# The mixture-of-experts layer of a two-block network on one core: four blocks of program joined into one, and the first weights loaded earlier

## The reference, cut to what matters

```python
h = h + expert_choice_ffn(rms_norm(h, norm2_w), w_router, w_gate, w_up, w_down)
h = rms_norm(h, final_norm_w)

def expert_choice_ffn(n, w_router, w_gate, w_up, w_down):
    cap = 2 * L // N_EXPERTS                                  # 64
    aff = softmax(einsum('bld,de->ble', n, w_router))         # over 16 experts
    vals, idx = lax.top_k(swapaxes(aff, 1, 2), cap)           # 64 tokens for each expert
    xs = n[idx]                                               # [16, 64, 1024]
    y = einsum(silu(einsum(xs, w_gate)) * einsum(xs, w_up), w_down) * vals[..., None]
    return zeros((L, D)).at[idx].add(y)
```

## Time and profile before

| what | value |
|---|---|
| median of 3 runs | 3746.36 us (3746.19 to 3746.59) |
| span of the profiled execution | 3742.8 us, of which 3.6 us less than the median of the runs |
| PE busy | 3347.0 us (89% of the span) |
| DVE, ACT, POOL busy | 1713.9, 1074.5, 305.7 us |
| read from HBM | 320.17 MB, 86 GB/s over the span |
| w_experts slabs | 96, of 1024 KB each |

### The profile page before, as it was taken

One profiled execution on the slowest core, in us unless ns is written; L12 is line 12 of the kernel. 1 busy time (PEld: TensorE's weight loads), 2 busy tenths in 40 slices (PEclk: granted clock), 3 DMA queues, 4 the chain that ended last, 5 costly groups with the idle time before them and its releaser, 6 DMA issues. The chain is left out here.

```text
span 3742.8 us, 39198 instructions
## 1 busy us (share of the span) xinstructions
PE 3347.0 (89%) x15374; PEld 2407.1 (64%) x15374; DVE 1713.9 (46%) x2459; ACT 1074.5 (29%) x1530; POOL 305.7 (8%) x260
## 2 busy tenths in 40 slices
PE   6999999879958776999998899998999998889997
PEld 3476574635744234888774468887888784568886
DVE  3758657556340014442436744423442326744433
ACT  3322231123220014222222632223222213642222
POOL 3212210012010001000002000000000002000001
PEclk8999999989969997999999999999999998999998
DMA  2101000000227972222310022222222311022221
GB/s 87 46 24 46 23 24 34 35 23 1 90 81 294 420 296 69 101 92 99 110 71 6 1 102 100 99 92 81 101 94 97 111 43 44 1 90 101 91 100 56
DMA packets 50838, 325.16 MB, mean 87 GB/s; under 512 B 7056, under 2 KB 7568, under 8 KB 13328
## 3 DMA queue, kind: packets, MB, share of 16 engines
q1 hardware_dynamic: 50704, 323.34, 23.0%
HBM read 320.17 MB, written 2.10 MB: 86 GB/s over the span
## 5 line engine op out<-in xcount | busy, mean ns | idle before, releaser
L364 PE MATMUL psum<-ffn_x_hi,ffn_w_hi 128*128 128x512 f32 x1408 | 548.2, 389 | 1.4 <-DVE ffn_x_lo L320 1.3
L364 PE MATMUL psum<-ffn_x_hi,ffn_w_lo 128*128 128x512 f32 x1408 | 547.7, 389 | 0.0
L364 PE MATMUL psum<-ffn_x_lo,ffn_w_hi 128*128 128x512 f32 x1408 | 547.7, 389 | 0.0
L309 DVE TENSOR_TENSOR ffn_w_lo<-ffn_raw,ffn_w_hi 128x2048 fp32r<-128x2048 f32 x128 | 293.4, 2292 | 420.3 <-ACT ffn_w_hi L280 420.3
L280 ACT ACTIVATE ffn_w_hi<-ffn_raw 128x2048 fp32r<-128x2048 f32 x128 | 245.2, 1916 | 564.3 <-PE psum L364 564.3
L104 PE MATMUL psum<-mix_normed,mix_ring 128*128 128x512 f32 x832 | 366.7, 601 | 13.0 <-DVE recurrences_work L1226 8.3
L364 PEld LDWEIGHTS psum<-ffn_x_hi,ffn_w_hi 128*128 128x128 f32 x1408 | 264.4, 188 | 61.8 <-DVE ffn_w_lo L316 6.8
L364 PEld LDWEIGHTS psum<-ffn_x_lo,ffn_w_hi 128*128 128x128 f32 x1408 | 264.4, 188 | 54.7
L364 PEld LDWEIGHTS psum<-ffn_x_hi,ffn_w_lo 128*128 128x128 f32 x1408 | 264.3, 188 | 54.6
L104 PEld LDWEIGHTS psum<-mix_normed,mix_ring 128*128 128x128 f32 x832 | 159.5, 193 | 214.3 <-issue 213.6
L364 PE MATMUL psum<-ffn_hid_hi,ffn_w_hi 128*128 (+1 forms) x704 | 273.9, 389 | 0.0
(11 more groups left out here) (477 smaller groups left out, 5407.9 us busy)
## 6 DMA issues: line engine op xcount, KB each, us to landing
ffn_raw<-w_ffn SPq DMA_DIRECT2D x128, 1024.0 KB, 4.8
mix_ring<-w_experts SPq DMA_DIRECT2D x48, 1024.0 KB, 13.6
mix_ring<-w_mix SPq DMA_DIRECT2D x32, 1024.0 KB, 7.5
mix_normed<-w_experts SPq DMA_DIRECT2D x24, 1024.0 KB, 13.6
experts_slabs<-w_experts SPq DMA_DIRECT2D x24, 1024.0 KB, 13.6
mix_ring<-w_gdn SPq DMA_DIRECT2D x16, 1024.0 KB, 4.9
mix_ring<-w_ssd SPq DMA_DIRECT2D x10, 1024.0 KB, 4.8
mix_ring<-w_out SPq DMA_DIRECT2D x7, 1024.0 KB, 7.4
```

The lines of the kernel that those rows point to most:

```text
L309: dve.tensor_tensor(w_lo[:, q, :], raw[:, q, :], w_hi[:, q, :].bitcast(F32), ALU.subtract)\
L364: ins = pe.matmul(out, wp[:, q, w], xp, start=start and a == 0, stop=stop and a == 2)
```

## The change

The stages `norm2`, `route`, `pick` and `experts` become one block, `experts`.

- **Norm.** The factor 1/rms is a number for each token. Where tokens lie on the partitions it is one column, `rstd` of 128x4. PE makes its sums by four products of one column (L1754); it is multiplied in where the turned tiles leave PSUM (L1836 on ACT, L1881 on DVE) and on the logits (L1885). ACT and DVE only multiply the residual's tiles by the gain, four each (L1828, L1869). The turning of the tiles (L1763) now comes ahead of the logits.
- **Picking in four groups.** `pick` is built and used for four experts (256 columns) at a time: DVE by 4 instructions of 128x256 a group (L1907), PE by 64 products of 256 columns (L1680). Group 0 comes ahead of the first pair. Groups 1 to 3 are cut in four parts of 16 products each, and `aside` puts two parts into each of the pairs 0 to 5. The turns for `put` go into the pairs 6 and 7 in the same way. The weighing stands between the gate and the up products of pair 0.
- **Eleven early slabs.** SP issues nine slabs at the start of the block: six into the ring and its extra slots, three into the memory of `y`, whose later rows aren't written until these are read. Two more follow into the memory of `m.xT` when the logits are done. The 85 others wait for `used` as before, on a ring of 8 slots.
- The buffers that only the mixer uses are given free ahead of the layer (`head_memory`), which makes the room. The scatter is the same.

The core of the diff:

```diff
-    with stage(nc, m, "route") as (block, sem):
...
-            for n in range(SLOTS):
-                fetch(sp, n)
...
-    with stage(nc, m, "pick") as (block, sem):
...
-                    for part in (x_hi, x_lo):
-                        ins = pe.matmul(m.ps[:, 4 + n % 4, :], part[:, t, tok(k)], pick[:, t, half * T:(half + 1) * T],
...
-        @block.sync
-        def _(sp):
-            for n in range(n_early, 12 * pairs):
-                if n >= slots:
-                    sp.wait_ge(used, (n - slots) // 2 + 1)
-                sp.dma_start(ring[n % slots], io["w_experts"][n]).then_inc(landed[n % slots], 16)
...
+    @block.sync
+    def _(sp):
+        sp.dma_start(router, io["w_router"]).then_inc(loaded, 16)
+        for n in range(n_first):
+            sp.dma_start(slots[n], io["w_experts"][n]).then_inc(landed[n], 16)
+        for n in range(n_over):
+            sp.dma_start(over[n], io["w_experts"][n_first + n]).then_inc(over_landed[n], 16)
+        sp.dma_start(m.rope_tables, io["const_f"][:, m.rope_at:m.rope_at + m.rope_width]).then_inc(tables, 16)
+        sp.wait_ge(logits, 1)
+        for n in range(n_first + n_over, n_early):
+            sp.dma_start(slots[slot(n)], io["w_experts"][n]).then_inc(landed[slot(n)], 16)
+        for n in range(n_early, 12 * pairs):
+            before = n - n_slots if n >= n_early + n_slots else \
+                slot(n) if slot(n) < n_first else slot(n) + n_over
+            sp.wait_ge(used, before // 2 + 1)
+            sp.dma_start(slots[slot(n)], io["w_experts"][n]).then_inc(landed[slot(n)], 16)
+        sp.wait_ge(tables, 16)
...
+        def gather(g, j, bank):
+            for k in (2 * j, 2 * j + 1):
+                for t in range(NT):
+                    for part in (x_hi, x_lo):
+                        ins = pe.matmul(m.ps[:, bank, k % 2 * wide:(k % 2 + 1) * wide], part[:, t, tok(k)],
+                                        pick[:, t, g * wide:(g + 1) * wide],
+                                        start=(t == 0 and part is x_hi), stop=(t == NT - 1 and part is x_lo))
+            ins.then_inc(gathered, 1)
+
+        def turn_picks(pair):
+            for t in range(NT):
+                ins = pe.transpose(m.ps[:, 7, tok(t)], pick[:, t, tok(pair)].bitcast(F32), m.ident)
+            ins.then_inc(put_done, 1)
+
+        def aside(i, spot):
+
+            if i < 2 * (groups - 1):
+                g, j = i // 2 + 1, 2 * (i % 2) + spot // 2
+                if spot == 0:
+                    pe.wait_ge(read_a, 2 + i)
+                    pe.wait_ge(picked, NT * (g + 1))
+                    gather(g, j, 7)
+                elif spot == 2:
+                    pe.wait_ge(read_v, 3 + i)
+                    gather(g, j, 7)
+                return
+            done = 2 * (i - 2 * (groups - 1))
+            if spot == 0:
+                pe.wait_ge(*((put_a, done) if done else (read_a, 2 * groups)))
+            elif spot < 3:
+                pe.wait_ge(put_v, done + spot)
+            else:
+                pe.wait_ge(put_a, done + 1)
+            turn_picks(2 * done + spot)
...
+        for t in range(NT):
+            ins = pe.matmul(m.ps[:, 7, t:t + 1], m.squares[:, tok(t)], m.ones[:, 0:1], start=True, stop=True)
+        ins.then_inc(summed, 1)
+        for n in range(2 * NT):
+            half, t = divmod(n, NT)
+            pe.wait_ge(x_by_act, 2 * half + 2)
+            pe.wait_ge(x_by_dve, 2 * half + 2)
+            if n >= 6:
+                pe.wait_ge(split, n - 5)
+            for k in range(4):
+                ins = pe.transpose(m.ps[:, turn_bank(n), tok(k)], m.xT[:, 4 * half + k, tok(t)], m.ident)
+            ins.then_inc(tok_turned, 1)
+        pe.wait_ge(loaded, 16)
+        for t in range(NT):
+            ins = product(pe, m.ps[:, 6, t * NE:(t + 1) * NE], lambda k: m.xT[:, k, tok(t)],
+                          lambda k: router[:, k, :])
+        ins.then_inc(logits, 1)
+        pe.wait_ge(normed, 1)
+        pe.wait_ge(split, 2 * NT)
+        for t in range(NT):
+            ins = pe.transpose(m.ps[0:NE, 0, tok(t)], affinity[:, t, :], m.ident)
+        ins.then_inc(aff_turned, 1)
+        pe.wait_ge(placed, 1)
+        for t in range(NT):
+            ins = pe.transpose(m.ps[:, 1, t * NE:(t + 1) * NE], chosen[:, tok(t)], m.ident[0:NE, 0:NE])
+        ins.then_inc(back, 1)
+        pe.wait_ge(picked, NT)
+        for j in range(4):
+            gather(0, j, 4 + j)
+        for i in range(pairs + 1):
+            if i < pairs:
+                if i >= 2:
+                    pe.wait_ge(hidden, i - 1)
+                for s in range(2):
+                    if i == 0:
+                        pe.wait_ge(read_v, s + 1)
+                        pe.wait_ge(read_a, s + 1)
+                    elif i % 2 == 0:
+                        pe.wait_ge(read_v, i + 2)
+                        pe.wait_ge(read_a, i + 2)
+                    gate_or_up(i, 0, s)
+                    aside(i, s)
+            if i == 0:
+                weigh()
+            else:
+                turn(i - 1)
+            if i < pairs:
+                for s in range(2):
+                    gate_or_up(i, 1, s)
+                    aside(i, 2 + s)
+            if i:
+                pe.wait_ge(turned_read, i)
+                if i >= 2:
+                    pe.wait_ge(y_read, i - 1)
+                for s in range(2):
+                    down(i - 1, s)
...
+            act.activation(x_hi[:, t, half * T:(half + 1) * T], m.ps[:, turn_bank(n), :], ACT.Copy,
+                           scale=rstd[:, t:t + 1]).then_inc(hi_done, 1)
...
+        def picks(g):
+            e = NE // groups
+            for t in range(NT):
+                dve.tensor_tensor(pick[:, t, g * wide:(g + 1) * wide].rearrange("p (e s) -> p e s", e=e),
+                                  m.slot.unsqueeze(1).to_broadcast([P, e, CAP]),
+                                  slot_of[:, t, g * e:(g + 1) * e].unsqueeze(2).to_broadcast([P, e, CAP]),
+                                  ALU.is_equal).then_inc(picked, 1)
+
+        picks(0)
+        for j in (0, 2):
+            take(0, j, 4 + j)
+        for g in range(1, groups):
+            picks(g)
+        for i in range(pairs):
+            if i < 2 * (groups - 1):
+                take(i // 2 + 1, 2 * (i % 2), 7)
...
-            resid_norm_stage(nc, m, "norm2", m.gains["norm2"], m.xT)
-            with expert_memory(nc, m):
-                experts(nc, m, io)
+            experts(nc, m, io)
```

More of the change, by code:

```diff
@@ L1775, in experts @@
-    picking.close()
-    y = slabs.enter_context(nc.sbuf_tensor("experts_y", [P, NE // 2, D], F32))
-    extra = parts.enter_context(nc.sbuf_tensor("experts_slabs", [P, 2, SLAB], F32))
-    ring += [extra[:, s, :] for s in range(2)]
-    hid, silu, hid_t = (cut(small, 2 * T * n, 2, T) for n in range(3))
-    slots = len(ring)
-    pairs = NE // 2
-    with stage(nc, m, "experts") as (block, sem):
-        landed = sem(slots)
-        used, silued, hidden, turned, turned_read, y_read = sem(6)
+    pairs, groups = NE // 2, NE // 4
@@ new lines, in experts, with sb, slot @@
+    wide = 2 * P
+    with ExitStack() as ctx:
+        def sb(what, *shape, dt=F32):
+            return ctx.enter_context(nc.sbuf_tensor(f"experts_{what}", [P, *shape], dt))
+        pick, tok_hi, tok_lo = (sb(what, 4096, dt=F32R) for what in ("pick", "tok_hi", "tok_lo"))
+        pick = cut(pick, 0, NT, NE * CAP)
+        x_hi, x_lo = (cut(buf, 0, NT, D) for buf in (tok_hi, tok_lo))
+        put = cut(tok_hi, 0, pairs, T)
+        y_hi, y_lo = (cut(tok_lo, 2048 * n, 2, pairs, P) for n in range(2))
+        gathered_x = sb("xs", 2 * KD * wide)
+        xs = [cut(gathered_x, g * KD * wide, KD, wide) for g in range(2)]
+        y = sb("y", pairs, D)
+        extra = sb("slabs", 2, SLAB)
+        small = sb("small", 4 * T + 320)
+        hid, hid_t = (cut(small, 2 * T * n, 2, T) for n in range(2))
+        silu = cut(m.norm_tmp, 0, 2, T)
+        rest, chosen, ones_row, count = (cut(small, T * n, T)[0:NE] for n in (2, 3, 0, 1))
+        at = 4 * T
+        affinity, slot_of, router = cut(small, at, NT, NE), cut(small, at + 64, NT, NE), cut(small, at + 128, KD, NE)
+        peak, total, rstd = (cut(small, at + 256 + 4 * n, NT) for n in range(3))
+        top, weight = cut(small, at + 272, 8)[0:NE], cut(small, at + 280, pairs)
+        spare = m.xT[:, :, :].rearrange("p k t -> p (k t)")
+        lent = y[:, :, :].rearrange("p i d -> p (i d)")
+        slots = [m.ring[:, s, :] for s in range(SLOTS)] + [extra[:, s, :] for s in range(2)] + \
+                [spare[:, s * SLAB:(s + 1) * SLAB] for s in range(2)]
+        over = [lent[:, (s + 1) * SLAB:(s + 2) * SLAB] for s in range(3)]
+        n_slots, n_over, n_first = len(slots), len(over), 6
+        n_early = n_slots + n_over
+        by_expert = lambda a: a.unsqueeze(2).to_broadcast([P, NT, NE])
+        def slot(n):
+            return n if n < n_first else n - n_over if n < n_early else (n - n_early) % n_slots
@@ L1788, in experts @@
```

(20 more changed lines are left out.)

448 lines of the change are left out of this document (181 added, 267 removed).

## The result

The changed kernel takes **3694.43 us** (median of 4 runs, 3688.53 to 3699.28), the kernel before in the same comparison 3746.28 us (3741.26 to 3746.59). The ratio is 0.9867 with the interval [0.9852, 0.9881], a gain of 51.9 us against the 51.1 that were forecast. The profiled execution took 3690.96 us, with a span of 3689.2. Run and span are thus 1.8 us apart, as in every other execution that has both; the 3.6 us given for the kernel before compare its span with the median of other executions.

A forecast was written before the change was run, and what follows sets the result against it. The layer was taken as a chain of small steps, then a stream bound by transfers. Used 6 at 1130.3 + 2.3 + 78 x 2.492 = 1327.0 instead of 1378.1, 51.1 us less: 3746.4 - 51.1 = 3695.3 us, range 3686 to 3709.

The forecast's parts named there:

- U6: End of the expert step on PE that raises `used` to 6, releasing slabs 18 and 19; forecast at 1130.3.
- softmax, picking, numbers: Between logits and picking matrix: 19.0 us before, plus one instruction of 0.23 us and two handovers, 19.3 us.
- picking matrix of group 0: DVE ahead of the gathering: 4 instructions of 256 columns at 0.4 us each, without a barrier, done at 1080.7.
- gathering of group 0: PE ahead of the first expert step: 64 products at 0.127 us plus 2.6 us for the clock, 10.7 us.
- weighing, and the step behind it: PE in pair 0, ahead of used 3: weighing 9.6 us, then a step of 3.55 us plus 1.8 for the clock.
- Turns: The 32 turns at the block's start, from 1043.5: their old 6.63 us, ending at 1050.1.
- Cold logits: Rival: the clock doesn't rise behind the turns, logits take 13.84 us instead of 9.6, 4.2 us more; chance 0.2.
- Serial loads: Rival: weight loads don't overlap in the gathering, 0.22 us a product, 11.8 us more, 3707.1 us; chance 0.12.
- The lower bound of 6.1 us: Least time for the logits' 32 products, all at clock 1.00, from 21 records in 2 us, two a product.
- the rival of the warm start: Logits and weighing both at 1.00 throughout, 3.5 us less each: 8.8 us less in all, 3686.5 us; chance 0.08.
- The idle queue: Between 1095.0 and 1130.3 the transfer queue moves only 7 slabs (17 us) and idles for some 16 us.
- 2.3 + 78 x 2.492 behind used 6: Stream's end: 2.3 us extra landing time, then 78 slabs left at 2.492 us each; last slab at 1327.0.

The follow-up runs named there:

- weigh one pair: Changed kernel with 28 of the weighing's 32 products left out, for timing only: 3684.71 us, layer 276.97 us.
- weigh spread: Changed kernel with the weighing cut into four runs of 8 products, one behind each gate and up step of pair 0: 3689.39 us, layer 281.71 us.
- narrow weighing: Changed kernel with the weighing in four runs and in reduced precision, affinities split into rounded part and rest: 3686.12 us, layer 278.77 us.
- the repeat: The changed kernel, unchanged, measured and profiled again: 3699.91 us, layer 287.79 us.
- eight early: Changed kernel with eight early slabs instead of eleven, none in the memory of y: 3701.18 us, layer 288.37 us.
- group 1 ahead: Changed kernel with the 64 gathering products of group 1 moved ahead of pair 0: 3695.91 us, layer 287.88 us.

## Why the prediction was right, and where it was off

**Right in its structure.** That the layer is a chain and then a stream, that the end is the moment from which the stream is full plus the slabs left, and that this moment is `used` at 6, all held. The experiments that moved U6 moved the layer with it (weigh one pair: 12.9 and 12.1; weigh spread: 6.5 and 7.3; narrow weighing: 10.4 and 10.3), and those that left U6 in place left the layer within the 1.2 us of the repeat (eight early, group 1 ahead). Step by step, in us from the block's start (the prediction's times less 1042.2):

| step | predicted | measured |
|---|---|---|
| end of the turns | 7.9 | 6.7 |
| logits | 9.6 | 9.26 |
| softmax, picking, numbers | 19.3 | 19.3 |
| picking matrix of group 0 | 1.6 | 1.43 |
| gathering of group 0 | 10.7 | 10.26 |
| first expert step | at 49.2 | at 47.0 |
| used 2 | at 58.4 | at 56.4 |
| weighing, and the step behind it | 9.6 + 5.35 | 11.09 + 6.44 |
| used 6 | at 88.1 | at 88.6 |
| last step behind used 6 | 196.7 | 200.5 |
| last step | at 284.8 | at 289.0 |

- *Turns.* I took their old 6.63 us; they took 5.14, since the clock rose within them (0.88 at 1040 to 1042).
- *Cold logits* is refuted. 9.26 us, at 1.00 first and 0.50 from 1048 on. The trace of before held this row already, as the weighing.
- *Serial loads* is refuted. The spacing is 0.12 us at 2.4 GHz, as forecast, so the load of new weights does lie beside the product before it. The Trainium skill, TensorE: Matmul & The Clock Gate, Part 3, The mechanism, says that it doesn't where the row group is the same. This trace disagrees with it for these products of 128x128: 0.12 us, not 0.21. Narrow products, in which little but the load is left, come every 0.11 us, so the load isn't short either, it is covered.
- *Weighing: the mis-sized term ahead of U6.* It came from 9.6 us of before, where the clock had stayed at 1.00 beyond 1140. Here it was at 0.50 by 1096, 4 us after the start, and the step behind paid 2.8 us instead of 1.8. Together 2.6 us more; the earlier first step hid it in the sum. How long the clock holds varies by execution: the second profile of this kernel has 10.87 and 4.98 us. The lower bound of 6.1 us was misread besides: the 21 records of a window of 2 us count those that reach into it from outside. They start 0.11 us apart, so 32 products at the full clock take 7.1 us, and the rival of the warm start is worth 2.5 instead of 3.5 us for each of its two runs.
- *The idle queue.* For 7 slabs (17 us) between 1095.0 and 1130.3 the prediction's own numbers give 18 us of idling, not 16; nothing rests on it.
- *The term that failed: 2.3 + 78 x 2.492 behind used 6.* It says 196.7; all nine profiles of the new order show 199.2 to 201.3, on average 3.5 us more. The 2.3 us hold: the slab that used 6 releases lands 4.7 us after its issue. What fails is that from there on a slab lands every 2.492 us. The issues of the slabs 18, 19 and 20 in the kernel after, each in a window of its own, and the transfers while slab 20 is due (columns as in rows 1):

```profile
mix_normed<-w_experts SPq DMA_DIRECT2D x1, 1024.0 KB, 4.7
mix_ring<-w_experts SPq DMA_DIRECT2D x1, 1024.0 KB, 6.9
mix_ring<-w_experts SPq DMA_DIRECT2D x1, 1024.0 KB, 7.4
1131.00:1132.00 1.00, 1.00 (x8) 0.38 (x6) 0.00 (x0) 0.27 (x1) 0.00 (x0) 1.00 0.85 139
```

Issued at 1124.39, 1124.77 and 1128.57, they land at 1129.1, 1131.7 and 1135.9. Slab 20 was issued 3.1 us before slab 19 landed and still comes 4.2 us behind it, 1.7 late. While it was due, the DMA engines had a busy share of 0.85 in one microsecond and moved only 139 GB/s. The slabs 30 and 40 are 0.9 and 0.6 us late and two others 0.3 together: 3.6 of the 3.8 us by which the term misses in this kernel. In seven of the other eight profiles it is the same, single slabs late by up to 1.7 us. Over these eight two thirds of the lateness lie among the slabs 19 to 23, just behind the restart. The ninth, with eight early slabs, is no counterexample. Its queue isn't empty at U6 (1128.08):

```profile
1126.00:1128.00 2.00, 2.00 (x10) 0.43 (x6) 0.00 (x0) 0.00 (x0) 0.00 (x0) 1.00 0.99 418
1128.00:1130.00 2.00, 2.00 (x14) 0.97 (x14) 0.69 (x1) 0.60 (x1) 0.00 (x0) 1.00 1.03 434
```

There slab 18 has to queue and lands 7.6 us after its issue, and behind it hardly a slab is late, which comes to the same 199.8. So the misses lie in single landings, mostly where the queue starts again; why those slabs are late stays open. The sum had the same fault before the change: used 1 at about 1154.6, 2.3 and 88 x 2.492 give 1376.2 there, and the last step began at 1378.10. Of these 1.9 us, 1.6 are one slab, number 17, which lands 4.04 us behind its predecessor in both profiles of that kernel. I could have seen them by trying the formula on the old kernel.

**Right in the total partly by luck.** The layer gained 4.2 us less than forecast, and the first comparison showed 0.8 more. The totals of both kernels scatter by 5 us and more around their medians, so the closeness of 51.9 to 51.1 is luck; that the gain is near 47 is not. The second comparison (43 us) misses on the other side. Both lie in the range.

## What to carry to other kernels

Where a queue of loads is released by the consumer, find the release from which the queue is full: everything on the consumer ahead of it costs its full time, and loads brought forward beyond what the queue could do while it idles are worth nothing. Side work in the first steps isn't hidden by the stream that it holds back; a long run of narrow products above all is better cut into short ones between wide steps (eight at a time here). Before a formula for a stream's end is used on the new kernel, try it on the old one: what it misses there it may miss again.

## What the runs showed of the hardware that was not expected

- PE's clock falls although PE is never idle. In the weighing PE was busy for 2.00 us of 2 and the clock went from 1.00 to 0.50. The same 32 products in four runs between wide steps kept it at 1.00 (7.6 us in the runs instead of 11.09, and 3.65 instead of 6.44 for the step behind).
- The 32 turns raised it from 0.50 to 0.88 and 1.00, with only eight narrow records and 4.22 us of idling ahead of them.
- In a stream that is otherwise even at one slab in 2.49 us, single slabs that were issued in time land up to 1.7 us late, two thirds of it just behind the point where the queue starts again. In the kernel after this is 3.6 us in all.
- The time of the whole program scatters by 0.2% to either side (the kernel before ran from 3738.61 to 3754.00 us over these comparisons) while that of the layer inside it repeats to 1.2 us or better (335.91 and 335.33; 289.03 and 287.79). For a change within one stage the profile is the finer instrument, if both ends are measured in the same execution; below some 2 us a single profile doesn't tell.
